# First stage of a hybrid decoder step taken block by block of k, with x in seven parts and the pool scales turned later

## The reference, cut to what matters

```
def rmsnorm(x, g):
    xf = x.astype(F32)
    var = jnp.mean(xf * xf, axis=-1, keepdims=True)
    return (xf * lax.rsqrt(var + RMS_EPS) * g.astype(F32)).astype(x.dtype)

def project(x, ln_g, w_in):
    """RMSNorm + single combined input projection, partitioned among all head groups."""
    B, T, _ = x.shape
    h = jnp.einsum('btd,dn->btn', rmsnorm(x, ln_g), w_in)
    ...
    q, k, v, g_a, qi, wi, ki, u, g_b = parts
```

## Time and profile before

| | |
|---|---|
| median of 3 runs | 2081.46 us (2081.32 to 2081.74) |
| the profiled execution, its own time | 2080.8 us |
| its span, first to last instruction | 2078.9 us |
| PE busy | 2064.7 us, 99% of the span |
| DVE, ACT, POOL busy | 1296.7, 735.1, 411.1 us |
| mean granted clock of TensorE | 0.999 |
| first product of segment qi | 46.70 us |

### The profile page before, as it was taken

One profiled execution on the slowest core, in us unless ns is written; L12 is line 12 of the kernel. 1 busy time (PEld: TensorE's weight loads), 2 busy tenths in 40 slices (PEclk: granted clock), 3 DMA queues, 4 the chain that ended last, 5 costly groups with the idle time before them and its releaser, 6 DMA issues. The chain is left out here.

```text
span 2078.9 us, 38867 instructions
## 1 busy us (share of the span) xinstructions
PE 2064.7 (99%) x14175; PEld 1972.1 (95%) x14175; DVE 1296.7 (62%) x1762; ACT 735.1 (35%) x917; POOL 411.1 (20%) x574
## 2 busy tenths in 40 slices
PE   9999999999999999999999999999999999999998
PEld 7888888999999999999999999999999999999998
DVE  5545545577777445666677767565565866655564
ACT  6433333323232333333333323333334433333333
POOL 1100100021210010235642103222222511111100
PEclk9999999999999999999999999999999999999999
DMA  8777776755554565666667657878777855555554
GB/s 233 207 221 215 219 210 205 214 167 160 156 160 138 181 192 167 182 192 175 198 187 216 175 157 231 243 246 261 246 246 248 259 169 168 167 162 166 157 166 148
DMA packets 341330, 406.03 MB, mean 195 GB/s; under 512 B 20332, under 2 KB 316204, under 8 KB 341000
## 3 DMA queue, kind: packets, MB, share of 16 engines
q1 hardware_dynamic: 293704, 291.75, 47.8%
q0 software_dynamic: 29968, 94.61, 14.7%
q10 hardware_dynamic: 17584, 18.70, 2.7%
HBM read 377.68 MB, written 31.45 MB: 197 GB/s over the span
## 5 line engine op out<-in xcount | busy, mean ns | idle before, releaser
L245 DVE TENSOR_TENSOR lo<-raw,hi 128x1024 fp32r<-128x1024 f32 x542 | 687.8, 1273 | 562.9 <-ACT hi L240 561.3
L269 PE MATMUL main<-XX,hi 128*128 128x320 f32 x3264 | 1029.2, 315 | 0.0
L271 PE MATMUL main<-XX,lo 128*128 128x320 f32 x3264 | 1008.8, 309 | 0.0
L270 PE MATMUL main<-XX,hi 128*128 128x320 f32 x3264 | 1008.3, 309 | 0.0
L240 ACT ACTIVATE hi<-raw 128x1024 fp32r<-128x1024 f32 x542 | 569.8, 1057 | 852.1 <-PE main L271 531.5
L269 PEld LDWEIGHTS main<-XX,hi 128*128 128x128 f32 x3264 | 613.1, 188 | 8.6 <-issue 5.0
L270 PEld LDWEIGHTS main<-XX,hi 128*128 128x128 f32 x3264 | 613.3, 188 | 2.3
L271 PEld LDWEIGHTS main<-XX,lo 128*128 128x128 f32 x3264 | 612.7, 188 | 0.0
L256 PE MATMUL main<-XX,hi 128*128 128x512 f32 x1024 | 355.9, 392 | 0.0
L257 PE MATMUL main<-XX,lo 128*128 128x256 f32 x1024 | 286.8, 280 | 0.0
L256 PEld LDWEIGHTS main<-XX,hi 128*128 128x128 f32 x1024 | 191.5, 187 | 42.5 <-issue 0.2
(11 more groups left out here) (302 smaller groups left out, 1557.3 us busy)
## 6 DMA issues: line engine op xcount, KB each, us to landing
raw<-w_in SPq DMA_DIRECT2D x416, 512.0 KB, 4.0
raw<-w_out SPq DMA_DIRECT2D x128, 512.0 KB, 3.7
deck<-cache_k POOLq DMA_DIRECT2D x64, 256.0 KB, 4.4
projT<-stg ACTq DMA_DIRECT2D x35, 320.0 KB, 3.0
keep<-cache_v POOLq DMA_DIRECT2D x40, 256.0 KB, 3.6
deck<-cache_v POOLq DMA_DIRECT2D x24, 256.0 KB, 3.6
deck<-maskD POOLq DMA_DIRECT2D x8, 516.0 KB, 5.4
ipg<-cache_idx_k POOLq DMA_DIRECT2D x64, 64.0 KB, 3.2
```

Of the source, the lines that this page charges most:

```text
L245: nc.vector.tensor_tensor(low, raw[:, slot, :, 0:width], high.bitcast(F32), ALU.subtract).then_inc(lo_ready, 1)
L269: nc.tensor.matmul(sums, wh, XH[:, k, :], start=first, stop=False)
L270: nc.tensor.matmul(sums, wh, XL[:, k, :], start=False, stop=False)
L271: mm = nc.tensor.matmul(sums, wl, XH[:, k, :], start=False, stop=last)
```

## The change

PE's list in the first stage is now written block by block: four blocks of x are turned, and then come the products of block k and the turning of block k + 4 in alternation. The three tiles of a block stand together, two of 128 tokens and one of 64. Each block's products wait for their own `XL`. The weight chunks are split behind single blocks (`SPLIT_AT`). x comes in seven parts: 256, 256, 512, 512, 512, 1024 and 1024 columns, of which SP and ACT ask for the first three. The first weight chunk is asked for in the place where the pool scales were, ahead of the second part of x. The pool scales are asked for by ACT, and turned with the bias products in segment qi. `WARM` is 12.

```
-            X_CUTS = [(0, XW // 2), (XW // 2, XW)] + [(i * XW, (i + 1) * XW) for i in range(1, 4)]
+            X_CUTS = [(0, XW // 4), (XW // 4, XW // 2), (XW // 2, XW), (XW, 3 * XW // 2), (3 * XW // 2, 2 * XW),
+                      (2 * XW, 3 * XW), (3 * XW, 4 * XW)]
...
-            WARM = 17
-
-            SPLIT_AFTER = [(c, ) for c in range(4)] + [(4, 5), (6, 7), (8, 9), (10, )]
+            WARM = 12
+
+            SPLIT_AT = (1, 5, 9, 13, 17, 19, 22, 25, 28, 30, 31)
...
-            def first_products(pe, c):
+            def first_products(pe, k):
+                c, kk = k // KK, k % KK
                 slot = c % SLOTS
                 pe.wait_ge(lo_ready, c + 1)
-                for kk in range(KK):
...
+                pe.wait_ge(s_xl, k + 1)
...
                 sp.dma_start(ident[:], t["c_ident"]).then_inc(s_small, 16)
                 sp.dma_start(gN[:], t["ln_g"][0].rearrange("(k p) -> k p", p=P)).then_inc(s_small, 16)
-                sp.dma_start(pscN[:], t["pool_scale"][0].rearrange("(k p) -> k p", p=P)).then_inc(s_small, 16)
+                first_chunk(0)
                 x_part(sp, 0, 1)
-                for c in range(SLOTS):
+                x_part(sp, 0, 2)
+                for c in range(1, SLOTS):
                     first_chunk(c)
...
-                for part in (2, 3, 4):
-                    pool.wait_ge(s_x[part - 2], 48)
+                for part in range(3, len(X_CUTS)):
+                    pool.wait_ge(s_x[part - 3], 48)
...
-                for part in range(2):
+                for part in range(3):
                     x_part(act, 1, part)
                     x_part(act, 2, part)
+                act.dma_start(pscN[:], t["pool_scale"][0].rearrange("(k p) -> k p", p=P)).then_inc(s_onehot, 16)
...
-                pe.wait_ge(s_small, 48)
-                nc.tensor.transpose(bank[0][:, 0:KT], gN[:], ident[0:KT, 0:KT])
-                nc.tensor.transpose(bank[0][:, KT:KT + POOLW // P], pscN[:],
-                                    ident[0:POOLW // P, 0:POOLW // P]).then_inc(s_gT, 1)
...
+                pe.wait_ge(s_small, 32)
+                nc.tensor.transpose(bank[0][:, 0:KT], gN[:], ident[0:KT, 0:KT]).then_inc(s_gT, 1)
+
+                def turn_tokens(k):
+                    pe.wait_ge(s_x[[a <= k * P < z for a, z in X_CUTS].index(True)], 48)
+                    if k >= 4:
+                        pe.wait_ge(s_xl, k - 3)
+                    for i, (c0, r) in enumerate(TT):
+                        tr = nc.tensor.transpose(sbank[k % 4][:, c0:c0 + r], xN[i][0:r, k * P:k * P + P], ident[0:r, 0:r])
+                    tr.then_inc(s_xT, 1)
+
+                for k in range(4):
+                    turn_tokens(k)
                 idle_products(3)
-                for c in range(CH):
-                    if c + 1 < CH:
-                        turn_tokens(c + 1)
-                    pe.wait_ge(s_xl, KK * (c + 1))
-                    first_products(pe, c)
+                for k in range(KT):
+                    first_products(pe, k)
+                    if k + 4 < KT:
+                        turn_tokens(k + 4)
...
+                        nc.tensor.transpose(sbank[0][:, 0:POOLW // P], pscN[:], ident[0:POOLW // P, 0:POOLW // P])
```

More of the change, by code:

```diff
@@ L472, in first_lo @@
                                         ALU.subtract).then_inc(lo_ready, 1)
-            def first_products(pe, c):
+            def first_products(pe, k):
+                c, kk = k // KK, k % KK
                 slot = c % SLOTS
                 pe.wait_ge(lo_ready, c + 1)
-                for kk in range(KK):
[L478 to L487, removed]
+                pe.wait_ge(s_xl, k + 1)
+                both = hi[:, slot, kk, 0:2 * IH]
+                wh, wl = hi[:, slot, kk, 2 * IH:WT], lo[:, slot, kk, 0:ID]
+                first, last = k == 0, k == KT - 1
+                nc.tensor.matmul(bank[2][0:2 * IH, 0:N], both, XH[:, k, :], start=first, stop=False)
+                nc.tensor.matmul(bank[2][0:2 * IH, 0:N], both, XL[:, k, :], start=False, stop=last)
+                nc.tensor.matmul(bank[3][:, 0:N], wh, XH[:, k, :], start=first, stop=False)
+                nc.tensor.matmul(bank[3][:, 0:N], wh, XL[:, k, :], start=False, stop=False)
+                mm = nc.tensor.matmul(bank[3][:, 0:N], wl, XH[:, k, :], start=False, stop=last)
+                if kk == KK - 1:
+                    mm.then_inc(chunk_used, 1)
             def square(act, n):
@@ L491, in square @@
                 r = TT[i][1]
-                for x_in in s_x[0:part + 2]:
-                    act.wait_ge(x_in, 48)
+                for x_in, (a, z) in zip(s_x, X_CUTS):
+                    if a < (part + 1) * XW and z > part * XW:
+                        act.wait_ge(x_in, 48)
                 if n:
@@ L559, in on_scalar @@
                                              scale=gT[:, k:k + 1]).then_inc(s_xh, 1)
-                    for a in SPLIT_AFTER[c]:
-                        if a < CH:
-                            first_hi(act, a)
-                        else:
-                            hi_chunk(act, a, a % SLOTS, 16 * (a // SLOTS + 1))
+                        for a in split_after(k):
+                            if a < CH:
+                                first_hi(act, a)
+                            else:
+                                hi_chunk(act, a, a % SLOTS, 16 * (a // SLOTS + 1))
                     if c:
@@ L592, in on_vector @@
                                                        XH[:, k, :].bitcast(F32), ALU.mult, ALU.subtract).then_inc(s_xl, 1)
[L593 to L597 removed]
+                        for a in split_after(k):
+                            if a < CH:
+                                first_lo(dve, a)
+                            else:
+                                lo_chunk(dve, a, a % SLOTS)
                 def finish(dve, q, j):
```

23 lines of the change are left out of this document (5 added, 18 removed).

## The result

| | before | changed |
|---|---|---|
| median of 8 runs, us | 2081.11 (2080.48 to 2081.74) | 2086.61 (2085.24 to 2090.32) |
| span of the profiled execution, us | 2078.9 | 2084.7 |
| PE busy, us | 2064.7 | 2071.6 |
| first product of qi, us | 46.70 | 52.00 |

The changed kernel takes 1.0028 of the time before (95% interval 1.0019 to 1.0037; the two medians alone give 5.5 us, 1.0026). That is slower by over 0.2%, if narrowly at the lower end of the interval, and 0.3 us above the upper end of the stated range (2086.3). The forecast was 2084.5. It started from 2081.46, the median of three runs; with eight the kernel before stands at 2081.11.

What follows compares the result with a forecast made beforehand. PE was taken to bound the kernel. First real product at 11.0, 28 blocks at 1.27 and a 2.9 us tail put qi at 49.5, 2.8 us later; with 0.2 for pool scales, 2084.5 us, range 2081.0 to 2086.3.

Steps and rivals of the forecast that it cites:

- The view that it rested on: PE, first stage: PE's time to the first product of qi reaches the kernel's end whole; 49.5 us predicted against 46.70.
- What a block costs: PE, first stage: entering and leaving the 64-row tile in every block makes a turned block 1.27 us instead of 1.08.
- rival without a price: 64-row tile in each block: weights load under products, a block costs 1.12 us, kernel 1.2 us faster (2080.3); chance 0.13.
- When P0 starts: PE's first real product (P0): at 11.0 us, bounds 10.0 and 12.0, against 12.86 before, held by x's second part.
- The clock: PE, less busy between 6 and 11 us: granted clock falls to half, loses 2.9 us, kernel at 2087.4; chance 0.05.
- Transfers late: Start of first stage: second or third part of x lands late behind the first weight chunk, kernel at 2086.5; chance 0.15.
- The sum: First stage plus pool scales: 11.0 + 28 x 1.27 + 2.9 = 49.5 us at qi, 2.8 later; with 0.2, 3.0 us more.

Runs made afterwards that it cites:

- before_rows128: Kernel before, with the 64-token tile turned as a full one of 128 rows (zeros in rows 64 to 127); median 2080.74 us, 0.9999 of before.
- before_warm12: Kernel before, with 12 products of zeros at the start instead of 17; median 2080.74 us, 1.0002 of the time before.
- rows128: Changed kernel, with the 64-token tile turned as a full one of 128 rows, zeros in rows 64 to 127; median 2083.43 us, 1.0014 of before.
- before_by_block: Kernel before, with the three tiles of a block standing together within each turn of four blocks; median 2092.76 us, 1.0052 of the time before.
- fill5: Changed kernel, with five more products of zeros between the second and third turned block; median 2087.16 us, 1.0030 of the time before.
- warm17: Changed kernel, with 17 products of zeros at the start instead of 12; median 2087.01 us, 1.0028 of the time before.
- old_turns: Changed kernel, with PE's old order of turns and products, the new loads kept; median 2083.97 us, 1.0015 of the time before.
- chunk0_later: Changed kernel, with the first weight chunk asked for behind the second and third parts of x; median 2088.72 us, 1.0037 of the time before.
- warm17_fill9: Changed kernel, with 17 products of zeros at the start and nine instead of three before the first block of products; median 2087.13 us, 1.0030 of before.
- rows128_chunk1_early: Changed kernel, with the 64-token tile padded to 128 rows, 17 products of zeros, weight chunk 1 asked for before x's third part; median 2084.09 us, 1.0011 of before.
- new_order_old_loads: Changed kernel, with x in five parts, the old transfer order (pool scales still late) and 17 products of zeros; median 2087.28 us, 1.0031 of before.
- rows128_six_pool_later: Changed kernel, 128-row tile, x in six parts, 17 products of zeros, POOL asking for each x part after the previous landed; median 2087.57 us, 1.0034 of before.
- rows128_old_loads: Changed kernel, 128-row tile, x in five parts, old transfer order (pool scales still late), 17 products of zeros; median 2081.61 us, 1.0005 of before.
- rows128_six_parts: Changed kernel, 128-row tile, 17 products of zeros, x in six parts, only the first weight chunk before x's second part; median 2081.11 us, 1.0001 of before.
- after_pool_later: Changed kernel, with POOL asking for each part of x only when the one before has landed; median 2091.02 us, 1.0052 of the time before.

## Why the prediction missed

**The view that it rested on** was right: one number, the first product of qi, carries the result. It moved by 5.3 us; the span by 5.8. Of the other 0.5, 0.16 are the pool scales (L256 behind the bias products starts 7.95 us after the first one instead of 7.79), predicted as 0.2, and 0.2 a wait for `XX` in the last stage. That wait is also in the profiles of before_rows128 and before_warm12, so it doesn't come from the change.

**What a block costs** was right in kind and low in size: 1.27 was predicted and 1.30 measured, 0.8 us over 28 blocks. The prediction took a value between 1.24 and 1.29; the price of a 64-row tile that stands alone was at the upper end, as the other place of its kind had said. That changes of tile are the cause of this term is shown by rows128 and before_by_block, one taking them away from the new kernel and one putting them into the old. The rival without a price is out.

**When P0 starts** was predicted at 11.0 and was 11.51. Its chain was the right one, the second part of x, at 9.12 (9.4 predicted). That ACT could begin the first `XH` at 7.2 was too early: its three last requests took 0.6, 0.8 and 1.2 us instead of 0.46, and the first `XH` began at 8.49; this cost nothing, as x came later still. The 0.5 us are the half clock. It lengthened the two turned blocks from 1.14 us to 1.49 and the three idle products from 0.64 to 0.90 (at 1.00 the first is read from fill5, the second from the 0.21 us at which its products of zeros follow each other), 0.6 us in all. At the whole clock x would have let P0 start at 9.12 + 1.14 + 0.64 = 10.9, and the weights, whose split ended at 10.96, at about 11.0. So some 0.5 of the 0.6 counts, and the predicted 11.0 would have been met, by the weights as narrowly as by x. The end of that split on DVE in the changed kernel:

```profile
10.68 0.28 DVE L476 TENSOR_TENSOR hi<-raw,hi 128x128 fp32r<-128x128 f32 x1
```

**The clock** was a rival with a chance of 0.05, on the ground that a gap of 1.40 us had been survived before. That was the step that failed: the sum put the clock at nothing. A gap of 1.22 us was followed by 3.4 us at half clock. Neither the gap nor the fewer zeros ahead of it explain that by themselves, as rows128 kept 1.00 with as few and with a gap of 1.44; the cause of the fall stays open. Behind P0 it cost 0.86 us in the first block (11.51 to 13.15 is 1.64 us for 0.78). With the 0.5 at P0, the 0.8 of the block price and 0.2 of a wait near 28 us that is 2.4 of the 2.5 us by which qi came later than the predicted 49.5. The kernel got 5.5 us slower where 3.0 were forecast, and of these 2.5 us about 1.4 are the clock and 0.8 a block price set too low. With the clock at 1.00 the result might have been in the range; but the sum also put the weights behind chunk 0 at nothing, and in warm17, where the clock held up to 18 us, PE waited 1.6 us for chunk 1 instead. Not all would have come back.

**Transfers late** was a rival for the third part of x. That part was in time, as were the later ones. Late were the weights, which the prediction followed only for chunk 0. In the changed kernel they cost PE just 0.2 us, because PE itself was late. (The 576 KB of x that this rival names are 512 KB of x and the 64 KB of the identity in SP's queue. And P0 at 12.0 with 1.29 a block gives 4.5 us more and 2086.0, not 4.6 and 2086.1. Neither moves the forecast.)

**The sum**, from the profiles: 28 blocks at 0.22 us more are 6.2 us, the half clock 1.4 us (0.5 ahead of P0 and 0.86 in the first block), the wait for chunk 3 0.2; gone are 2.0 us of waits for x and for the last `XL` (1.55 before 17.34 and 0.46 at the last chunk); and the start without the half clock gained 0.5. That is 5.3, as measured.

## What to carry to other kernels

Before matmuls of different row counts are interleaved, read the start-to-start steps at one change of tile, and multiply by the number of changes of the new order. Padding the small tile to full rows may be cheaper than leaving and entering (here 0.25 us for three full transposes against 0.51). A finer order that starts earlier brings no time if the loads behind it can't follow: count for every consumer, weights too, when it will now be needed. In the first microseconds a gap on PE can cost more behind it than it is long (1.22 us here, and 1.4 lost), but not every gap does. And before a single profile is explained, see how its time and mean granted clock lie among the other executions of the same kernel.

## What the runs showed of the hardware

- A 64-row transpose that stands between two transposes of 128 rows and a 128-row product adds 0.24 us over one padded to 128 rows (a block of 1.30 us in the changed kernel, 1.06 in rows128). The Trainium skill, TensorEngine Tiling (Array Packing), section Key Properties, says that a change of tiling mode drains the engine. The runs agree that the change costs time, and give its price here; the drain itself no row shows.
- The granted clock fell to half in the first 35 us in the profiles of the changed kernel and of old_turns, warm17, chunk0_later, fill5, warm17_fill9, rows128_chunk1_early, new_order_old_loads and rows128_six_pool_later, always behind or inside a gap of about 1.0 us or more on PE, and for about 3.4 us or about 7. It did not fall behind gaps of 1.40 us (before), 1.44 and 1.39 us (rows128), 1.56 us (before_warm12), 1.55 us (rows128_old_loads), 1.79 us (rows128_six_parts) and 2.3 us (after_pool_later). The gap's length alone doesn't tell, and the program alone doesn't either, as the two groups of new_order_old_loads show; what does stays open.
- In the profile of before_by_block all 1024 pairs of segment qi took 0.353 us instead of 0.347, at a granted clock of 1.00; 6.4 us in all. Its products of 512 columns, by line (min/median/max ns), where all other profiles have a median of 391:

```profile
L256 PE MATMUL main<-XX,hi x1024: 393/398/504, 50.8 to 416.9; 128*128 128x512 f32 x171
```

The program of that segment is the same. The profiled execution took 2091.74 us; another took 2087.62 and two took 2093.77 and 2094.94, so it may come and go between executions. Its cause is not known.
